# Low parts of sixteen weight pairs a layer by accumulating DMA, and two indexer blocks moved one group ahead

## The reference, cut to what matters

```
h = x * (1 + sc1) + sh1
q, k, v, qi, ki, wi, xr, yg = split(h @ w_in)            # 512 columns each, ki 64, wi 8
idx_score[t, s] = sum over 8 heads of relu(qi[t] . ki[s]) * wi[t]   # causal
sel = top_k(idx_score, 128)          # per query; attention only over these keys
attn = softmax(q . k over sel) @ v   # 4 heads of 128
lru = rg_lru(conv4(xr)) * gelu(yg)   # gates: sigmoid of block-diagonal products
x = layer_norm(alpha*x + (1+g1) * (concat(rms(attn), rms(lru)) @ w_out))
h2 = x * (1 + sc2) + sh2
x = layer_norm(alpha*x + (1+g2) * (relu(h2 @ w_up)^2 @ w_down))
```

## Time and profile before

| What | us |
|---|---|
| three runs | 1410.07, 1405.91, 1403.70 |
| the profiled execution's own time | 1405.28 |
| span of its trace | 1403.6 |
| PE busy | 1306.1 |
| DVE busy | 804.7 |
| ACT busy | 550.8 |
| POOL busy | 98.5 |

### The profile page before, as it was taken

The page is one execution under the profiler, slowest core; times in us unless marked ns, Lnnn a source line. Parts: engine busy times, 40 slices in busy tenths (PEclk is TensorE's granted clock), DMA queues, the critical chain, the costliest instruction groups (busy, mean ns, idle before and its releaser), DMA issues.

```text
span 1403.6 us, 17026 instructions
## 1 busy us (share of the span) xinstructions
PE 1306.1 (93%) x6225; PEld 1024.6 (73%) x6225; DVE 804.7 (57%) x1322; ACT 550.8 (39%) x849; POOL 98.5 (7%) x107
## 2 busy tenths in 40 slices
PE   3999797799999999999999997968999999999996
PEld 2777474577788888888867765647868888888886
DVE  3746779745763634636465557995565344253453
ACT  3833446532731423314346342555355133241331
POOL 3100002002000000000120000010100000000012
PEclk8999998899999999999989998979989999999998
DMA  9753334201235242343245342520213333323221
GB/s 315 242 189 121 105 120 165 91 30 61 76 105 160 94 150 90 104 154 101 75 136 175 126 135 91 179 76 1 90 31 114 100 101 91 104 90 105 90 75 60
DMA packets 73397, 158.56 MB, mean 113 GB/s; under 512 B 6528, under 2 KB 10872, under 8 KB 73336
## 3 DMA queue, kind: packets, MB, share of 16 engines
q1 hardware_dynamic: 59904, 108.61, 24.7%
q0 software_dynamic: 12800, 48.76, 10.4%
q10 hardware_dynamic: 632, 0.39, 0.1%
HBM read 155.64 MB, written 2.10 MB: 112 GB/s over the span
## 4 chain that ended last, share of the span: by engine, by line
PE 80%; DVE 15%; issue 2%; DMA 2%; ACT 1%; POOL 0%; POOLq 0%; DVEq 0%; SPq 0%; ACTq 0%
PE bank L634 23%; PE bank L635 23%; PE bank L636 23%; DVE idx_acc L1594 3%; DVE best L1592 3%; DVE w_lo L1408 2%; PE bank L679 2%; DMA first_mod<-in_w_mod_dram 2%; PE bank L599 1%; PE bank L537 1%; PE bank L852 1%; PE bank L731 1%; PE bank L832 1%; DVE turned_ring L1545 1%; PE bank L889 1%
## 5 line engine op out<-in xcount | busy, mean ns | idle before, releaser
L1408 DVE TENSOR_TENSOR w_lo<-w_raw,w_hi 128x1024 fp32r<-128x1024 f32 (+1 forms) x216 | 236.8, 1112 | 352.7 <-ACT w_hi L968 352.7
L968 ACT ACTIVATE w_hi<-w_raw 128x1024 fp32r<-128x1024 f32 (+1 forms) x216 | 202.7, 959 | 474.6 <-PE bank L636 473.1
L634 PE MATMUL bank<-a_hi,w_hi 128*128 128x512 f32 x896 | 371.4, 415 | 10.9 <-DVE a_lo L1450 7.0
L635 PE MATMUL bank<-a_lo,w_hi 128*128 128x512 f32 x896 | 352.8, 394 | 0.0
L636 PE MATMUL bank<-a_hi,w_lo 128*128 128x512 f32 x896 | 352.7, 394 | 0.0
L634 PEld LDWEIGHTS bank<-a_hi,w_hi 128*128 128x128 f32 x896 | 170.6, 190 | 64.4 <-issue 23.7
L634 PE MATMUL bank<-b_hi,w_hi 128*128 128x512 f32 x512 | 199.7, 390 | 0.0
L635 PEld LDWEIGHTS bank<-a_lo,w_hi 128*128 128x128 f32 x896 | 170.6, 190 | 39.2 <-issue 3.9
L636 PE MATMUL bank<-b_hi,w_lo 128*128 128x512 f32 x512 | 199.2, 389 | 0.0
L635 PE MATMUL bank<-b_lo,w_hi 128*128 128x512 f32 x512 | 199.2, 389 | 0.0
L636 PEld LDWEIGHTS bank<-a_hi,w_lo 128*128 128x128 f32 x896 | 170.3, 190 | 36.5
(11 more groups left out here) (267 smaller groups left out, 1457.3 us busy)
## 6 DMA issues: line engine op xcount, KB each, us to landing
mod_raw<-in_w_mod_dram POOLq DMA_DIRECT2D x40, 1024.0 KB, 6.2
w_raw<-in_w_up_dram SPq DMA_DIRECT2D x64, 512.0 KB, 3.7
w_raw<-in_w_down_dram SPq DMA_DIRECT2D x64, 512.0 KB, 3.7
w_raw<-in_w_in_dram SPq DMA_DIRECT2D x48, 512.0 KB, 4.2
w_raw<-in_w_out_dram SPq DMA_DIRECT2D x16, 512.0 KB, 6.0
first_mod<-in_w_mod_dram SPq DMA_DIRECT2D x4, 1024.0 KB, 19.5
first_mod<-in_w_mod_dram POOLq DMA_DIRECT2D x4, 1024.0 KB, 15.0
x_in<-in_x_dram POOLq DMA_DIRECT2D x4, 512.0 KB, 14.4
```

The costliest lines, as they stand in the source:

```text
L634: mm(o, wh, hi(kk), start=first, stop=False)
L635: mm(o, wh, lo(kk), start=False, stop=False)
L968: last = af(hi, src, ACT.Copy)
L1408: last = tt(lo, src, hi.bitcast(F32), ALU.subtract)
```

## The change

Four groups (k, q, yg, out0), 16 pairs a layer, get their low part in another way. ACT writes `w_hi` as before and also writes the negated high part to `w_lo`. Then POOL issues a DMA from `raw[:, p]` to `w_lo[:, p]` that adds to what is there, waits for it, and raises `lo_split`. DVE's subtraction of these pairs is gone. The adds stand in POOL's list among the loads of w_mod: pairs 0 and 1 of a group behind load n (5, 7, 9, 11), pair 2 behind load n+1, pair 3 ahead of load n+2.

Block 2 of the indexer moves from group k to the second half of v, block 3 from q to k. ACT's and DVE's lists are rewritten to match: convolution, topk rounds and adds interleave in a new order, and topk has done 45 rounds ahead of the attention loop where it had done 39.

```
+DMA_LO = ("k", "q", "yg", "out0")
...
+                def add_raw(name, p):
+                    g = group_at(name, l)
+                    n = l * len(DMA_LO) * PAIRS + DMA_LO.index(name) * PAIRS + p
+                    pool.wait_ge(hi_split, g * PAIRS + (p + 1))
+                    pool.dma_start(w_lo[:, p, :, :].bitcast(F32), raw[:, p, :, :], accum_op=ALU.add).then_inc(lo_added, 16)
+                    pool.wait_ge(lo_added, 16 * (n + 1))
+                    pool.wait_ge(lo_split, g * PAIRS + (PAIRS + p))
+                    pool.sem_inc(lo_split, 1)
                 for n in range(LATE_PAIRS):
+                    if 7 <= n <= 13 and n % 2:
+                        add_raw(DMA_LO[(n - 7) // 2], 3)
                     pool.wait_ge(mod_used, l * MOD_PAIRS + (NEXT_PAIRS + n + 1 - MR))
                     pool.dma_start(mod_raw[:, n % MR, :, :], ...
+                    if 5 <= n <= 11 and n % 2:
+                        add_raw(DMA_LO[(n - 5) // 2], 0)
+                        add_raw(DMA_LO[(n - 5) // 2], 1)
+                    if 6 <= n <= 12 and n % 2 == 0:
+                        add_raw(DMA_LO[(n - 6) // 2], 2)
...
# TensorE
                 group("v", l, a_high, a_low, nothing, between={
-                    **{2 * h + 1: idx_head(1, h) for h in range(IDX_HEADS)}, HALF: lambda: late_mod(l, 4)})
+                    **{2 * h + 1: idx_head(1, h) for h in range(IDX_HEADS)},
+                    **{HALF + 2 * h + 1: idx_head(2, h) for h in range(IDX_HEADS)}, HALF: lambda: late_mod(l, 4)})
                 group("k", ...
-                    **{4 + 3 * h: idx_head(2, h) for h in range(IDX_HEADS)}, HALF + 1: lambda: late_mod(l, 6)})
+                    **{4 + 3 * h: idx_head(3, h) for h in range(IDX_HEADS)}, HALF + 1: lambda: late_mod(l, 6)})
-                group("q", l, a_high, a_low, nothing, between={
-                    **{2 * h + 1: idx_head(3, h) for h in range(IDX_HEADS)}, HALF: lambda: late_mod(l, 8)})
+                group("q", l, a_high, a_low, nothing, between={HALF: lambda: late_mod(l, 8)})
...
# ScalarE, in split_hi
-                for src, hi, _ in pair_views(name, p):
+                for src, hi, lo in pair_views(name, p):
                     last = af(hi, src, ACT.Copy)
+                    if name in DMA_LO:
+                        last = af(lo, src, ACT.Copy, scale=-1.0)
...
# ScalarE, the list of the v and k groups
+                for p in range(PAIRS - 1):
+                    idx_relu(1 + p // 2, range(p % 2 * 4, p % 2 * 4 + 4))
+                    split_hi("k", l, p)
+                idx_relu(2, range(4, 8))
+                v_out_first()
+                split_hi("k", l, PAIRS - 1)
                 for p in range(PAIRS):
-                    split_hi("k", l, p)
-                    if p == PAIRS - 2:
-                        v_out_first()
-                v_out()
+                    for m in ((0, 1), (2,), (3,), ())[p]:
+                        vt_out(m)
+                    idx_relu(3, (2 * p, 2 * p + 1))
+                    if p < PAIRS - 1:
+                        split_hi("q", l, p)
...
-                slot(l, "q", k_out)
-                idx_relu(3)
+                k_out()
+                split_hi("q", l, PAIRS - 1)
...
# VectorE
             def split_lo(name, l, p, c=None):
+                if name in DMA_LO:
+                    return
                 g = group_at(name, l, c)
+                if name == "out1" and p == 0:
+                    ve.wait_ge(lo_split, g * PAIRS + PAIRS)
...
                 slot(l, "v", (none, none, none))
-                idx_add(1)
-                slot(l, "k", (lambda: (conv(0), conv(1)), lambda: (conv(2), conv(3)), lambda: (masks(), topk(4))))
-                idx_add(2)
+                idx_add(1, range(0, 4)); idx_add(1, range(4, 8)); conv(0); conv(1)
+                idx_add(2, range(0, 4)); conv(2); idx_add(2, range(4, 8)); conv(3)
+                masks()
+                for p, rounds_ in enumerate((4, 8, 13, 18)):
+                    topk(rounds_)
+                    idx_add(3, (2 * p, 2 * p + 1))
+                topk(20)
...
-                slot(l, "q", (lambda: topk(8), lambda: topk(12), lambda: (topk(15), k_out())))
-                idx_add(3)
+                topk(22)
-                slot(l, "yg", (lambda: topk(19), lambda: topk(23), lambda: (topk(26), q_out())))
-                slot(l, "out0", (lambda: topk(30), lambda: topk(34), lambda: topk(39)))
+                slot(l, "yg", (k_out, lambda: topk(28), lambda: topk(34)))
+                topk(36)
+                slot(l, "out0", (q_out, lambda: topk(41), lambda: topk(45)))
...
-                    topk(min(39 + u + 1, 3 * per))
+                    topk(min(45 + u + 1, 3 * per))
```

More of the change, by code:

```diff
@@ L274, in trunk_kernel @@
         pair_used = sem("pair_used")
+        lo_added = sem("lo_added")
         mod_in = [sem(f"mod_in{s}") for s in range(MR)]
@@ L1090, in idx_relu @@
                 def idx_relu(i, heads=range(IDX_HEADS)):
-                    if i == 1:
+                    if (i, heads[0]) == IDX[0]:
                         act.wait_ge(a_lo_s, l * 2 * DK + (DK + 2))
@@ L1098, in idx_relu @@
                         af(rel[:, u % 2, 0:(i + 1) * P], banks[b][:, 0:(i + 1) * P], ACT.Relu).then_inc(free_s[b], 1)
-                idx_relu(1)
                 def yg_out():
@@ L1111, in v_out_first @@
                         af(ring[:, ring_of("v", m), :], banks[m][:, :], ACT.Copy).then_inc(free_s[m], 1)
[L1113 to L1117, removed]
                 def vt_out(m):
@@ L1563, in layer, with idx_add @@
                 tt(ki_b[96:P, :], straight[32:64], swapped[32:64], ALU.subtract).then_inc(rope_done, 1)
-                def idx_add(i):
-                    if i == 1:
+                def idx_add(i, heads):
+                    if (i, heads[0]) == IDX[0]:
                         ve.wait_ge(free_s[4], uses_before(4, "wi", l) + 1)
-                    for h in range(IDX_HEADS):
+                    for h in heads:
                         u = IDX.index((i, h))
@@ L1625, in layer @@
                 slot(l, "v", (none, none, none))
-                idx_add(1)
-                slot(l, "k", (lambda: (conv(0), conv(1)), lambda: (conv(2), conv(3)), lambda: (masks(), topk(4))))
-                idx_add(2)
+                idx_add(1, range(0, 4))
+                split_lo("k", l, 0)
+                idx_add(1, range(4, 8))
+                conv(0)
+                split_lo("k", l, 1)
+                conv(1)
+                idx_add(2, range(0, 4))
+                split_lo("k", l, 2)
+                conv(2)
+                idx_add(2, range(4, 8))
+                conv(3)
+                masks()
+                split_lo("k", l, 3)
+                for p, rounds_ in enumerate((4, 8, 13, 18)):
+                    topk(rounds_)
+                    idx_add(3, (2 * p, 2 * p + 1))
+                    if p < PAIRS - 1:
+                        split_lo("q", l, p)
+                topk(20)
+                split_lo("q", l, PAIRS - 1)
                 def lru_input(m):
```

## The result

The changed kernel takes 1434.37 us (median of 4 runs, 1432.76 to 1437.47) against 1405.93 us: a ratio of 1.0201, 95% interval [1.0172, 1.0231]. It is 28.4 us slower, 14.2 us a layer. I had forecast 1385 us with a range up to 1428.

The account below looks back on a forecast made before the run. TensorE (PE) was taken as the bound, with time to win only where it stands still. A layer wins 11.9 - 2.3 - 0.95 + 4.0 - 2.3 = 10.3 us, two 20.7, from 1405.3 to 1385 us; range 1368 to 1428.

Parts of the forecast that it names:

- What bounds the kernel now: Whole kernel: PE bounds, busy 93%; q has a hole of 8.81 us from DVE's late add, then low clock.
- The groups on TensorE: Groups v to yg: v 31.9, k 32.3, q and yg 23.6 us each; 11.9 us in q goes.
- DVE keeps up: Groups v and k: DVE loses 19.5 us of subtractions a layer and adds scores in time; cost taken as 0.
- The attention loop: Loop after the groups: six fewer topk rounds take 8.7 us off DVE; half counted, 4 us, bounds 0 and 8.7.
- POOL's list: POOL's queue: adds hold up w_mod loads and the squares of lru_a; squares 2.3 us late a layer.
- 45.7 + 9A: When POOL comes free after v's end, from q's pair 3: 9 adds and 6 issues of 0.9, against 99.6 us.
- A: Time an add holds POOL, from issue to landing: taken as 5.9 us, range 3.6 to 11.8.
- Rival 1: POOL's chain of adds overruns before the squares: a loss from A = 7.4, 1417 us at A = 8; chance 0.33.
- Rival 2: ACT becomes the bound, its copies of k, q and yg 1 us later each: 1393 us; chance 0.10.
- The 0.95 charged for ACT at the gates: Before the first gate sigmoid: out0's pair 3 on ACT stands ahead and costs 0.95 us a layer.
- Rival 3: The hole moves to v or k, 8.8 us comes back and TensorE's clock drops: 1398 us; chance 0.10.
- Rival 4: Adds are quick, A under 5, and the loop gains its full 8.7 us: 1371 us; chance 0.05.

Follow-up runs that it names:

- the moves alone: The changed kernel with no adds by DMA, all low parts by DVE's subtraction, moved indexer blocks and new lists kept: 1378.26 us, ratio 0.9793.
- without the hold: The changed kernel with POOL not waiting for its adds; PE and SP wait for each add's own semaphore: 1375.27 us, repeated 1374.41.
- small loads: The changed kernel with w_mod loads 6 to 15 of each layer cut to 128 KB, POOL still held by each add: 1383.96 us, ratio 0.9846.
- with copies: The changed kernel with a plain copy in place of each accumulating DMA, so w_lo holds raw weights: 1415.74 us, ratio 1.0064.

## Why the prediction was wrong

*What bounds the kernel now* was right: the hole in q, its cause and its size. The kernel with the moves alone has no such wait.

*The groups on TensorE* were right. I wrote v 31.9, k 32.3, q 23.6 + 2.3. Found, between the marks: v 96.53 to 129.08 = 32.6, k 130.06 to 162.21 = 32.2, q 163.19 to 187.45 = 24.3. From v's end to the first scores I had told 96.4; without the hold it is 95.1, in the changed kernel 118.7. Q's wait for ACT's copies was 0.68 us in the trace, where I had charged 2.3.

*DVE keeps up*: right, and more than right. The kernel with the moves alone shows that DVE did not need the relief to close the hole. I had not asked that question: I gave the adds a part in a gain that the moves bring alone.

*The attention loop*: 4.0 us a layer was low. Without the hold the gain is 15.3 to 15.8 a layer, against my 12.65 before lateness. Of the 3 us, 1.6 is the wait in q. In layer 0 the loop takes 50.3 us from the first scores to the product behind it (224.54 to 274.85), where before it took 57.8 (233.25 to 291.02): 7.5 us less, near the upper bound of 8.7, and some of it is given back behind the loop.

*POOL's list* is the step that failed, in the line "From there POOL has 9 adds and 6 issues of 0.9": 45.7 + 9A. I took A as 5.9 us for every add, and it was 9.2 in the mean. The mechanism was named, and so was what would be late, but its size was wrong. A load of 1 MB was charged its issue and nothing more. It is in flight with the add that follows, and POOL waits for that add. Without such a load A was low by less: 5.9 told, 5.2 found in k and 6.6 to 7.1 in the chain. (My lower estimate of 4.4 us, by which the squares would not be late, is near the shortest landing, 4.5, and below every hold.)

The start of the chain agrees in the number and not in the reason: q's pair 3 was told at 128.4 + 40.3 = 168.7, when ACT has split it, and issued at 169.63. ACT had split it by 168.2; what POOL waited for was q's pair 2, which stood behind a load and held it 11.25 us. The 8 us of slack that I gave each add in k and in the first three pairs of q were used up by then. From there to the squares at 257.80 are 88.2 us; less 5.4 for the issues that is 9.2 us an add. The sum with 5.9 has the squares at 227.2, and 0.9 + 9 x (9.2 - 5.9) = 31 us is what they came later. About 25 us of it are the four adds behind a load (12.1 us in the mean), 5 us the five others (6.9). With small loads they start at 227.99.

My sum said the right thing about steepness: 9 us a layer for each us of A. With A = 9.2 the formula gives 29 us of lateness and a loss of 16 us a layer, and 14.2 were measured. A term with that slope needed its A from the worst place in the list. Rival 1 had the turning point, A = 7.4, and a reason, "the adds share the DMA engines with SP's loads". I looked for disturbance in SP's loads and in single long landings of 8.4 us. That reason is good for the 5 us; the 25 come from POOL's own loads, which the change itself puts in front of half of the adds. Load 10, too, the rival had late from A = 8.4 on, and it did come late, with loads 11 and 12.

Rival 2 (ACT the bound) is seen nowhere: after the change TensorE waits 0.6 to 0.7 us for ACT's copies. The 0.95 charged for ACT at the gates is there: TensorE's wait for the first of ACT's gate results was 0.83 us before and is 1.77 without the hold. Rival 3 (the hole moves) is not seen either: in k PE is busy throughout. Rival 4 is near what the kernel does without the hold, though with adds of 5.3 us to landing. Its 1371 us is not the range's lower end of 1368, which no line of the prediction works out.

On two of the prediction's pages. The Trainium skill, Collectives: The Full Stack, section The bandwidth ceiling, says that a reduction is paid for by its second source. The queue that POOL uses took 10.6% of 16 engines x 1376.5 us without the adds, 17.3% of 1373.6 us with them and 13.4% of 1414.3 us with copies; over 32 transfers that is 2.9 us of all engines for an add and 1.4 for a copy of the same 512 KB. Twice the time fits two sources read for one, so the trace agrees with the Trainium skill there, though it can't tell the second read from the addition. On the hold that the Trainium skill tells of in SBUF — State Buffer, section Who interferes with whom: the adds' issues took 847 to 933 ns over a layer, so none waited out a VectorE instruction; no run here shows such a hold. The prediction's bound of 7.1 us was not the rule's either: the instruction of 1.2 us is a TENSOR_TENSOR, and that section of the Trainium skill says that tensor_tensor was not seen to stall a DMA.

## What to carry to other kernels

A wait in an engine's list costs what stands behind it in that list, not what it waits for: before moving work to DMAs, give each its own semaphore and let the consumers wait, or count the whole chain against its deadline. A transfer that sets out behind a large one can last as long as both: here 5.2 us for the add and 5.9 for the load apart, and 11 to 13 together. And when a change has two parts, ask of each what the other leaves for it: here one part alone brought 28 of the 31 us.

## What the runs showed of the hardware

- An accumulating DMA of 512 KB within SBUF landed 4.5 to 6.0 us after its issue (median 5.0) with small transfers ahead (small loads, layer 0), and up to 12.4 with 1 MB loads ahead (the changed kernel). A plain copy's shortest was 2.8 us.
- It took 2.9 us of the 16 engines' time (worked out above), a copy 1.4, and its issue on POOL 0.85 us against 0.54.
- A 1 MB load in flight made an add 2 to 4 us longer also when it was issued from another engine's queue, and was itself slow: it landed after 9.8 us in the median (140 to 262 us), where POOL's loads had taken 5.9 before the change.
